# Recurrent layer: gates and keys in three groups of heads, gates ahead of the row splits, low part of the second rows behind the first scaling

## The reference, cut to what matters

```python
def hgrn2_mixer(h, w_in, lower_bound, g_norm_w, w_out):
    q, f, i, g = jnp.split(h @ w_in, 4, axis=-1)
    lb = lower_bound.astype(jnp.float32).reshape(HG_HEADS, HG_DIM)
    fg = lb + (1.0 - lb) * jax.nn.sigmoid(heads(f))
    o = hgrn2_chunkwise(jax.nn.silu(heads(q)), 1.0 - fg, heads(i), jnp.log(fg))
    ...
```

## Time and profile before

| what | us |
|---|---|
| median of 3 runs (lowest to highest) | 1408.45 (1407.83 to 1408.49) |
| the profiled execution, its own time | 1409.36 |
| its span, from first to last instruction | 1407.6 |
| TensorE busy in the span | 1326.5 (94%) |
| VectorE busy | 758.9 (54%) |
| ScalarE busy | 548.5 (39%) |
| GpSimd busy | 118.5 (8%) |

### The profile page before, as it was taken

How to read it: one execution, slowest core, us unless ns; L and a number is a source line. 1 busy time by engine, 2 the same in 40 slices (tenths; PEclk the granted TensorE clock), 3 DMA queues, 4 the chain that set the end, 5 groups by cost and what they waited for, 6 DMA issues and landing times.

```text
span 1407.6 us, 20789 instructions
## 1 busy us (share of the span) xinstructions
PE 1326.5 (94%) x8168; PEld 973.4 (69%) x8168; DVE 758.9 (54%) x1432; ACT 548.5 (39%) x996; POOL 118.5 (8%) x131
## 2 busy tenths in 40 slices
PE   8989999999798999999979898999999988999997
PEld 7767444343686744344459786699997874999985
DVE  3976212112688631111264795687775655478766
ACT  5554111111446321121144232166654453366552
POOL 1030000000003100000030450310000021000000
PEclk9999999999899989999989999999999999999999
DMA  9439899999724779999995239745765510555740
GB/s 308 148 119 369 353 420 421 421 420 395 243 76 180 309 320 420 421 420 421 421 335 180 90 120 120 235 131 181 245 225 185 182 60 1 190 186 186 248 148 30
DMA packets 130136, 347.83 MB, mean 247 GB/s; under 512 B 10288, under 2 KB 86342, under 8 KB 105476
## 3 DMA queue, kind: packets, MB, share of 16 engines
q1 hardware_dynamic: 125232, 332.29, 62.7%
q0 software_dynamic: 3952, 13.74, 4.3%
q10 hardware_dynamic: 868, 0.63, 0.1%
HBM read 342.44 MB, written 4.19 MB: 246 GB/s over the span
## 4 chain that ended last, share of the span: by engine, by line
PE 75%; DVE 12%; DMA 4%; SPq 4%; ACT 2%; issue 2%; POOL 0%; DVEq 0%; ACTq 0%
PE bank L1938 11%; PE bank L1769 8%; PE bank L1771 8%; PE bank L1770 8%; PE bank L1949 6%; PE bank L1673 5%; SPq L642 4%; DMA slot<-in_w_up 4%; PE bank L1781 4%; PE bank L2256 3%; PE bank L2260 3%; PE bank L2258 3%; PE bank L2139 2%; PE bank L1713 1%; PE bank L1960 1%
## 5 line engine op out<-in xcount | busy, mean ns | idle before, releaser
L1769 PE MATMUL bank<-x_high,w_high 128*128 128x256 f32 x1024 | 291.1, 284 | 2.3 <-DVE w_low L1213 2.3
L1770 PE MATMUL bank<-x_low,w_high 128*128 128x256 f32 x1024 | 289.7, 283 | 0.0
L1771 PE MATMUL bank<-x_high,w_low 128*128 128x256 f32 x1024 | 289.7, 283 | 0.0
L774 ACT ACTIVATE w_high<-slot 128x1024 fp32r<-128x1024 f32 x214 | 215.5, 1054 | 183.7 <-PE bank L1771 86.2
L1938 PE MATMUL bank<-slot,arena 128*64 128x512 f32 x976 | 223.0, 592 | 1.5 <-DMA slot<-in_w_up 1.5
L1769 PEld LDWEIGHTS bank<-x_high,w_high 128*128 128x128 f32 x1024 | 196.5, 192 | 4.5 <-issue 4.4
L1770 PEld LDWEIGHTS bank<-x_low,w_high 128*128 128x128 f32 x1024 | 196.5, 192 | 0.1
L1771 PEld LDWEIGHTS bank<-x_high,w_low 128*128 128x128 f32 x1024 | 196.5, 192 | 0.0
L1938 PEld LDWEIGHTS bank<-slot,arena 128*64 128x64 f32 x976 | 73.3, 137 | 142.5 <-issue 142.2
L1570 DVE TENSOR_TENSOR w_low<-slot,w_high 128x1024 fp32r<-128x1024 f32 x88 | 103.8, 1222 | 61.3 <-ACT w_high L774 61.0
L774 ACT ACTIVATE arena<-bank 128x512 f32<-128x512 f32 (+7 forms) x130 | 60.4, 495 | 167.1 <-PE bank L2023 85.1
(11 more groups left out here) (299 smaller groups left out, 2216.7 us busy)
## 6 DMA issues: line engine op xcount, KB each, us to landing
slot<-in_w_gate SPq DMA_DIRECT2D x62, 1024.0 KB, 19.6
slot<-in_w_up SPq DMA_DIRECT2D x60, 1024.0 KB, 18.9
slot<-in_w_down SPq DMA_DIRECT2D x60, 1024.0 KB, 18.7
slot<-in_ffn_w_in SPq DMA_DIRECT2D x44, 1024.0 KB, 7.6
slot<-in_ffn_w_out SPq DMA_DIRECT2D x22, 1024.0 KB, 5.0
slot<-in_hgrn_w_in SPq DMA_DIRECT2D x16, 1024.0 KB, 7.0
slot<-in_w_in SPq DMA_DIRECT2D x10, 1024.0 KB, 9.8
slot<-in_w_o SPq DMA_DIRECT2D x8, 1024.0 KB, 5.0
```

Of the source, the lines that this page charges most:

```text
L774: return nc.scalar.activation(dst, src, ACT.Copy)
L1769: mm(dst, high[:, k, :], x_high[:, k, :], start=(k == 0), stop=False)
L1770: mm(dst, high[:, k, :], x_low[:, k, :], start=False, stop=False)
L1771: last = mm(dst, low[:, k, :], x_high[:, k, :], start=False, stop=(k == KD - 1))
```

## The change

It has three parts. ScalarE takes the sigmoid of each pair of f before it makes the high part of rows, for the pairs 2 and 3; for the pairs 0 and 1 the order stays. VectorE makes gates and keys in three groups (heads 0 to 3, 4 and 5, 6 and 7), each with a key instruction of its own that counts `keys_ready`. `low_rows(0)` stands behind the second group, and `low_rows(1)` behind the scaling of level 0, ahead of its merges. TensorE waits for the first group ahead of the first half of the heads in level 0, and for all three ahead of the second.

```diff
@@ -1012,9 +1012,9 @@
                     if i < 2:
                         split_slot(2, names[i + 6], i + 6)
-                    else:
+                    drained(nc.scalar.activation(C["Pd"][:, 2 * i:2 * i + 2, :], b[:, :].rearrange("p (c n) -> p c n", c=2), ACT.Sigmoid), (2, f"hf{i}"))
+                    if i >= 2:
                         split_rows(i - 2)
-                    drained(nc.scalar.activation(C["Pd"][:, 2 * i:2 * i + 2, :], b[:, :].rearrange("p (c n) -> p c n", c=2), ACT.Sigmoid), (2, f"hf{i}"))
@@ -1490,15 +1490,17 @@
-                low_rows(0)
-                for h in range(HG_HEADS):
-                    if h % 2 == 0:
-                        evacuated(dve, (2, f"hf{h // 2}"))
-                    last = V.tensor_scalar(C["Pd"][:, h, :], C["Pd"][:, h, :], lb[:, 3, h:h + 1], lb[:, 2, h:h + 1], ALU.mult, ALU.add)
-                link(last)
-                V.tensor_scalar(C["K"], C["Pd"], -1.0, 1.0, ALU.mult, ALU.add).then_inc(sem("keys_ready"), 1)
-                dve.wait_ge(sem("keys_ready"), 1)
-                low_rows(1)
+                for first, n in ((0, 4), (4, 2), (6, 2)):
+                    some = slice(first, first + n)
+                    for h in range(first, first + n):
+                        if h % 2 == 0:
+                            evacuated(dve, (2, f"hf{h // 2}"))
+                        last = V.tensor_scalar(C["Pd"][:, h, :], C["Pd"][:, h, :], lb[:, 3, h:h + 1], lb[:, 2, h:h + 1], ALU.mult, ALU.add)
+                    link(last)
+                    V.tensor_scalar(C["K"][:, some, :], C["Pd"][:, some, :], -1.0, 1.0, ALU.mult, ALU.add).then_inc(sem("keys_ready"), 1)
+                    if first == 4:
+                        low_rows(0)
+                dve.wait_ge(sem("keys_ready"), 3)
@@ -1532,6 +1534,8 @@
+                    if li == 0:
+                        low_rows(1)
                     if li == len(LEVELS):
                         weigh_gates(0)
                     merge(li)
@@ -2127,7 +2131,7 @@
                         if li == 0:
-                            pe.wait_ge(sem("keys_ready"), 1)
+                            pe.wait_ge(sem("keys_ready"), (1, 3)[s])
```

## The result

| | us |
|---|---|
| changed kernel, median of 5 runs (lowest to highest) | 1402.32 (1398.23 to 1404.60) |
| kernel before, median of 5 runs (lowest to highest) | 1408.49 (1407.83 to 1410.26) |
| ratio, with its 95% interval | 0.9949 (0.9933 to 0.9966) |
| profiled execution, its own time and its span | 1404.60 and 1402.8 |

The kernel is faster by about half a per cent. The median is the forecast, 1402.3. So the range was too narrow for what the runs do. Two later sets of runs of the same kernel gave 0.9954 and 0.9959. The stage itself did what was forecast, and the profile shows it.

The account below looks back on a forecast made before the run. TensorE bounds the levels, after waiting 4.6 us for keys at level 0 and losing 1.9 to low clock. Level 1 starting at 784.55, not 790.72, gains 6.17; 6.2 from 1408.45 gives 1402.3 us, range 1401.6 to 1404.3.

Parts of the forecast that it names:

- The earlier start: TensorE at level 0: first half starts at 775.16, second at 777.25, level 1 at 784.55, gaining 6.17 us.
- S: Stretch from the start of f's last matmul to level 1's start on TensorE; forecast 6.17 us shorter.
- the short gap: TensorE between level 0's halves: a gap of 0.35 us that leaves the clock alone.
- the term for it: TensorE in level 0: 1.9 us of the stretch before the change was put down to the low clock.
- VectorE behind the first scaling: Moved low part ends 784.5, first merge 785.1, 1.2 us to spare; level 1's scaling 0.5 late, no TensorE wait.
- The moved pair: VectorE's low part of the second rows, moved behind level 0's scaling beside GpSimd: forecast to take 3.43 us.
- the 2.4 to 3.5: Sign of being right in the profile after: the moved pair on VectorE takes 2.4 to 3.5 us.
- rival (a): GpSimd blocks both halves of VectorE's moved low part; TensorE waits 1.2 us for L110's bank: 1403.5 us, chance 0.10.
- The row of 3.43: VectorE's slowest low-part pair in the levels, with GpSimd running too; used to price the moved pair at 3.43.
- Rival (b): No early first half: level 0 begins at 777.25 in one piece, 4.5 us gained, 1404.0 us; chance 0.08.
- (c): Stages behind are held by something that doesn't move; all or nearly all is lost, 1407 to 1408.5 us; chance 0.06.
- (d): VectorE becomes the bound of the levels through added GpSimd blocks: 3.2 us slower, 1411.6 us; chance 0.04.

Follow-up runs that it names:

- e5: Kernel before, with 19 identity products filling TensorE's wait for the keys ahead of level 0: median 1406.72 us, ratio 0.9986.
- e3: Changed kernel, but TensorE waits for all three key groups ahead of both halves of level 0: median 1403.31 us, ratio 0.9960.
- e6: Changed kernel with ScalarE's old order, high parts of rows ahead of the sigmoids: median 1403.93 us, ratio 0.9965.
- e2: Kernel before with only the sigmoids moved ahead of the high parts of rows: median 1405.45 us, ratio 0.9977.
- e8: Changed kernel with 20 identity products in TensorE's wait for the norm ahead of the recurrent layer: median 1401.66 us, ratio 0.9950.
- e1: Changed kernel run again, unaltered: median 1402.50 us, ratio 0.9954.
- e10: Changed kernel unaltered, a third time, beside the kernel before on the same chip: median 1402.66 us, ratio 0.9959.
- e4: Changed kernel with the low part of the second rows back ahead of the first scaling: median 1403.58 us, ratio 0.9958.
- e7: Changed kernel with 9 and 11 identity products in TensorE's two idle stretches behind the levels: median 1401.67 us, ratio 0.9952.
- e9: Changed kernel with identity products behind the levels and 16 ahead of the norm's transposes: median 1401.82 us, ratio 0.9956.

## Why the prediction was right or wrong

**The earlier start, right.** Forecast and profile of the changed kernel:

| step | forecast | profile |
|---|---|---|
| keys of heads 0 to 3 done | 769.4 | 769.34 |
| keys of heads 4 and 5 done | 771.4 | 771.46 |
| first low part done | 773.8 | 773.73 |
| keys of heads 6 and 7 done | 777.20 | 777.22 |
| level 0 starts | 775.16 | 775.19 |
| level 1 starts | 784.55 | 784.62 |
| S shorter by | 6.17 | 6.13 |

The 128x512 keys take 0.43 (0.47 forecast), the 128x1024 keys 0.69 (0.72). The clock stayed up after the short gap; the term for it was 1.9 in the text and is 1.76 by level 0 to level 1 of before (10.80 against 9.04), which e5's 1.65 bears out. The total was read from the two starts, so this slip moved nothing.

**VectorE behind the first scaling, right in its outcome, mis-sized.** The moved pair was put at 3.43 us and took 4.52. That is also outside the 2.4 to 3.5 that the prediction would have taken as a sign of being right. The merges began at 785.46 instead of 784.5, and the first is done at 786.19, where TensorE wants its bank at 784.62 + 1.75 = 786.37: 0.2 us to spare, not 1.2. Level 1's scaling came 1.3 late, not 0.5. So rival (a), which put the end of the pair at 786.8 and the wait at 1.2, was near: the pair ended at 785.53. GpSimd's rows show why: it got an instruction in ahead of each half of the pair.

```profile
780.62 1.37 POOL L744 TENSOR_TENSOR arena<-arena 128x512 f32<-128x512 f32 x1
781.95 2.50 POOL L743 TENSOR_TENSOR arena<-arena 128x512 f32<-128x512 f32 x1
784.52 1.91 POOL L744 TENSOR_TENSOR arena<-arena 128x512 f32<-128x512 f32 x1
```

Between 781.01 and 785.53 VectorE's pair needs 2.36 by itself, so 2.2 us went to GpSimd: its halves take 2.06 and 2.54 instead of about 1.2 each, and end 1.1 us behind GpSimd's instructions that end at 781.99 and 784.45. The Trainium skill, "SBUF — State Buffer", section "Who interferes with whom", has it that such a pair of instructions shuts one another out whole, and these rows agree. The row of 3.43 was the wrong one to take: only one of its halves met GpSimd (the second, 2.31 us from 809.65 in the trace of before). VectorE had time enough later and no wait came of it.

**Rival (b)** was run as e3: 11.37, with the clock kept, 1.8 above the changed kernel. It was priced at 4.5 won, and won 15.68 - 11.37 = 4.31. **Rivals (c) and (d)** fell: the levels are unchanged and nothing was given back by a later wait. The 1.34 us that one profile lost later is not such a wait.

**The range, wrong.** By the ratio the measured time is 1401.3 us, 0.3 below the range's low end of 1401.6. The step that failed is the one on that low end: "the runs' spread of about 0.3". It was read off three runs, 1407.83 to 1408.49. Sixty runs of the kernel before, in four sets, reach from 1404.76 to 1413.43, and seventeen of the changed one from 1398.23 to 1404.60. Their means are 1408.78 and 1402.28, 6.5 us apart; with standard deviations of 1.9 and 1.7 that is uncertain by about 0.9. So the stage's 6.13 and the ratios agree, and a set of five runs can miss by over 1 us either way. That the median of five fell on 1402.3 to the tenth is luck for the same reason; what bears the forecast out is S. A range of 1401.6 to 1404.3 priced the rivals and left the draw of the runs out. The two profiled executions show the same draw: their spans differ by 4.8 us, not by the stage's 6.1.

## What to carry to other kernels

Where TensorE waits for a chain over two engines, cut the chain's last link into the pieces that TensorE uses first, and take urgent short work ahead of long work with cover; price it from the start of the last matmul ahead to the first evenly spaced one behind. Idle time costs twice if the clock falls behind it, as behind the 4.6 us here. Judge such an edit by its own stretch in the profile, and take the range for the whole from the spread of many runs, not of three.

## What was not expected of the hardware

Gaps of 1.92 us (e3, ahead of level 0) and 2.02 (e6, between its halves) left the clock at 1.00; gaps of 2.72 (e2) and 4.61 (before) ahead of it brought it to 0.62 and 0.53. Each was seen in one profile, and the gap alone doesn't decide. Behind 2.04 us of idle time at 858 us the clock was 0.52 in the changed kernel:

```profile
858.40:862.40 4.00, 1.79 (x8) 1.39 (x8) 3.60 (x7) 1.27 (x3) 0.00 (x0) 0.52 1.00 122
```
```profile
858.37 1.82 PE L2188 MATMUL bank<-ident,arena 128*128 128x128 f32 x8 [2.04 <-DVE arena L1565]
```

In the kernel before, the same eight matmuls behind the same gap ran at full speed:

```profile
864.47 1.10 PE L2184 MATMUL bank<-ident,arena 128*128 128x128 f32 x8 [2.04 <-DVE arena L1561]
```

Ten profiles have this gap unfilled (2.03 or 2.04 us). The eight matmuls take 1.06 to 1.10 us in four of them (before, e2, e5, e8), 1.77 to 1.82 in three (the changed kernel, e1, e10), and 1.26 to 1.66 in three (e3, e4, e6). The sixteen matmuls behind the next gap take 8.5 to 9.5 us in all ten, against 7.1 in e7 and e9. So the clock falls here in every execution, but sooner in one than in another. What decides that was not tested, and a gap of 2 us that left the clock alone in one profile, as in e3 and e6, need not do so in the next.

GpSimd can be shut out for longer than one instruction of VectorE's. One of its instructions on the decays, 1.0 to 1.9 us elsewhere, took 4.62 us in the levels of the changed kernel, while VectorE ran two halves of a low part and two scalings back to back, and VectorE then waited 1.17 us for it:

```profile
803.36 4.62 POOL L744 TENSOR_TENSOR arena<-arena 128x512 f32<-128x512 f32 x1
```
```profile
803.29 2.34 DVE L1490 TENSOR_TENSOR w_low<-slot,w_high 128x1024 fp32r<-128x1024 f32 x2
805.55 0.68 DVE L1535 TENSOR_TENSOR arena<-arena 128x512 f32<-128x512 f32 x1
806.15 0.68 DVE L1536 TENSOR_TENSOR arena<-arena 128x512 f32<-128x512 f32 x1
808.00 1.63 DVE L1535 TENSOR_TENSOR arena<-arena 128x512 f32<-128x512 f32 x1 [1.17 <-POOL arena L744]
```

This cost TensorE nothing, as its level had time to spare.
